# A two-layer hybrid trunk in fp32: five places where loads, transposes, decays, tokens and operand halves are reordered

## What is computed

```python
# layer 0
h = rmsnorm(x, even_norm_mix)
proj = h @ w_in                      # columns: bg, cg, hv, z, xbc, dt
y_a = bg * causal_dwconv(cg * hv, conv_w)
xbc = silu(causal_dwconv(xbc, ssd_conv_w) + ssd_conv_b)
dt = softplus(dt_raw + dt_bias); a = -exp(a_log)
y = ssd_scan(xs, dt, a, bm, cm) + d_skip * xs      # decays exp(cumsum(dt * a))
y_b = group_rmsnorm(y * silu(z)) * ssd_norm_g
x = x + concat(y_a, y_b) @ w_out
x = x + swiglu(rmsnorm(x, even_norm_ffn), w_gate, w_up, w_down)
# layer 1
x = x + diff_attention(rmsnorm(x, odd_norm_mix), ...)
h = rmsnorm(x, odd_norm_ffn)
logits = h @ w_router                # 8 experts, top 2 of them per token
x = x + sum over a token's two experts of gate * swiglu(h, w_e)
```

## Time and profile before

| | us |
|---|---|
| median of 3 runs | 2041.79 (2039.48 to 2042.93) |
| profiled execution, its own time | 2043.4 |
| its span, first to last instruction | 2041.6 |
| PE busy in it | 1971.8 (97%) |
| DVE, ACT, POOL busy | 749.8, 652.1, 490.9 |
| mean granted TensorE clock | 0.983 of full |

### The profile page before, as it was taken

How to read it: one execution, slowest core, us unless ns; L and a number is a source line. 1 busy time by engine, 2 the same in 40 slices (tenths; PEclk the granted TensorE clock), 3 DMA queues, 4 the chain that set the end, 5 groups by cost and what they waited for, 6 DMA issues and landing times.

```text
span 2041.6 us, 28889 instructions
## 1 busy us (share of the span) xinstructions
PE 1971.8 (97%) x11899; PEld 1731.5 (85%) x11899; DVE 749.8 (37%) x1138; ACT 652.1 (32%) x1061; POOL 490.9 (24%) x246
## 2 busy tenths in 40 slices
PE   7999999999999999998899999999999999999996
PEld 6787778888888888886688999999999999888885
DVE  4625564210010005948722000010010101989896
ACT  4333223232222224337630000000000011878784
POOL 3446664265445544540011000000000000000010
PEclk9999999999999999999898999999999999999998
DMA  7862222243233232330007977888888898999995
GB/s 241 298 197 74 63 73 93 73 124 93 92 95 103 88 105 75 101 104 1 22 1 268 322 241 260 300 299 302 276 305 288 284 312 278 377 372 374 361 396 212
DMA packets 295087, 405.38 MB, mean 199 GB/s; under 512 B 11264, under 2 KB 211018, under 8 KB 294954
## 3 DMA queue, kind: packets, MB, share of 16 engines
q1 hardware_dynamic: 292650, 395.11, 57.4%
q0 software_dynamic: 2304, 8.39, 1.1%
HBM read 372.67 MB, written 30.80 MB: 198 GB/s over the span
## 4 chain that ended last, share of the span: by engine, by line
PE 88%; DVE 3%; ACT 2%; DVEq 2%; POOL 2%; issue 1%; DMA 1%; SPq 0%; POOLq 0%; ACTq 0%
PE ps L1729 20%; PE ps L1736 10%; PE ps L375 5%; PE ps L376 5%; PE ps L377 5%; PE ps L393 5%; PE ps L394 5%; PE ps L395 5%; PE ps L1787 4%; PE ps L1789 4%; PE ps L1788 4%; PE ps L410 2%; PE ps L412 2%; PE ps L411 2%; DVEq L1186 1%
## 5 line engine op out<-in xcount | busy, mean ns | idle before, releaser
L1022 POOL TENSOR_TENSOR w_lo<-raw,w_hi 128x1024 fp32r<-128x1024 f32 (+1 forms) x159 | 390.3, 2463 | 462.7 <-ACT w_hi L758 462.7
L1563 DVE TENSOR_TENSOR s_lo<-s_raw,s_hi 128x1024 fp32r<-128x1024 f32 x198 | 236.9, 1222 | 28.1 <-ACT s_hi L1933 22.6
L2183 DVE TENSOR_TENSOR hid<-ps,silu_g 128x160 f32<-128x160 f32 x110 | 35.7, 324 | 550.1 <-ACT silu_g L1908 550.1
L1729 PE MATMUL ps<-xT,w_gate 128*128 128x132 f32 (+1 forms) x1760 | 226.6, 282 | 4.6 <-issue 4.0
L758 ACT ACTIVATE w_hi<-raw 128x1024 fp32r<-128x1024 f32 (+1 forms) x159 | 164.8, 1043 | 205.1 <-PE ps L395 136.4
L375 PE MATMUL ps<-act_a_hi,w_hi 128*128 128x512 f32 x568 | 226.3, 398 | 0.0
L1729 PE MATMUL ps<-xT,w_up 128*128 128x132 f32 (+1 forms) x1760 | 224.4, 281 | 0.0
L1908 ACT ACTIVATE silu_g<-ps 128x160 f32<-128x160 f32 x110 | 33.5, 304 | 593.3 <-PE ps L1729 593.3
L1933 ACT ACTIVATE s_hi<-s_raw 128x1024 fp32r<-128x1024 f32 x198 | 206.7, 1061 | 51.0 <-PE ps L1789 46.5
L377 PE MATMUL ps<-act_a_hi,w_lo 128*128 128x512 f32 x568 | 221.2, 389 | 0.0
L376 PE MATMUL ps<-act_a_lo,w_hi 128*128 128x512 f32 x568 | 221.1, 389 | 0.0
(11 more groups left out here) (355 smaller groups left out, 2949.1 us busy)
## 6 DMA issues: line engine op xcount, KB each, us to landing
w_gate<-in_moe_w_gate SPq DMA_DIRECT2D x55, 1024.0 KB, 5.6
w_up<-in_moe_w_up SPq DMA_DIRECT2D x55, 1024.0 KB, 8.5
w_down<-in_moe_w_down SPq DMA_DIRECT2D x55, 1024.0 KB, 11.0
s_raw<-in_moe_w_gate SPq DMA_DIRECT2D x33, 1024.0 KB, 7.6
s_raw<-in_moe_w_up SPq DMA_DIRECT2D x33, 1024.0 KB, 8.3
s_raw<-in_moe_w_down SPq DMA_DIRECT2D x33, 1024.0 KB, 7.7
raw<-in_even_w_in SPq DMA_DIRECT2D x43, 512.0 KB, 4.5
raw<-in_attn_w_qkv SPq DMA_DIRECT2D x24, 512.0 KB, 3.8
```

The lines of the kernel that those rows point to most:

```text
L1022: pool.tensor_tensor(w_lo[:, u % HL_SLOTS, 0:size(u)], raw[:, u % RAW_SLOTS, 0:size(u)], flat(w_hi[:, u % HL_SLOTS, 0:size(u)]), ALU.subtr ...
L1563: return eng.tensor_tensor(s_lo[u % S_HL][:], s_raw[u // 2 % S_RAW][:, u % 2, :], s_hi[u % S_HL][:].bitcast(F32), ALU.subtract)
L1729: mm = pe.matmul(ps[:, bank, i * CAP:i * CAP + width], w_slots[s][i][:, k, c:c + P], xT[:, k, 0:width], start=(k == 0), stop=(k == KD - 1))
```

## The change

**First loads.** Order now: tile 0 of x, gain, tile 1, units 0 and 1, the three `rows_sb` and three `small` loads, tile 2, unit 2, tile 3, unit 3. The transpose of `rows_sb` moves behind the two turns, ahead of unit 0's products, in another bank of PSUM (the accumulator memory); unit 3 waits until DVE has copied it. **Time steps.** The turn of `dt_rows` moves from ahead of the z units to between the first and the second. **Log decays.** `log_decays(c, 0)` and `(c, 1)` for c >= 1 move from the start of even a to the odd a before, ahead of `ssd_second`. **Home of the tokens.** `h_tok` moves to byte 81920 (that of `raw`), and other tiles are placed around it; DVE waits for all of `lo_done` before it writes there; SP's wait ahead of slot 3 goes, and a wait for the scatter comes one round later, ahead of the load of the next expert's rows; POOL's scatter waits for five hidden tiles and not three. **Last parts.** In the narrow passes the high and low parts of the last hidden chunk come right after its turn may be done, ahead of the parts of the weights that follow.

```diff
-    h_tok, _ = place("h_tok", [P, NT, D], F32, NT * D * 4)
+    h_tok, _ = place("h_tok", [P, NT, D], F32, 5 * NT * D * 4)
...
         load_x(0)
-        for src, r, n in rows:
-            sp.dma_start(rows_sb[r:r + n, :], src).then_inc(rows_in, 16)
         sp.dma_start(gain[:], gains[0][0].partition_broadcast(P)).then_inc(gain_in, 16)
         load_x(1)
-        for i, name in enumerate(("ssd_dt_bias", "ssd_a_log", "ssd_d")):
-            sp.dma_start(small[:, 16 * i:16 * i + 16], t[name][0].partition_broadcast(P)).then_inc(small_in, 16)
+
+        def load_rows_and_small():
...
         for u in range(N_UNITS):
             load(u)
-            if u < NT - 2:
-                load_x(2 + u)
+            if u == 1:
+                load_rows_and_small()
+            if 1 <= u < NT - 1:
+                load_x(1 + u)
...
         pe.wait_ge(masks_ready, 1)
-        pe.wait_ge(rows_in, 48)
-        pe.transpose(ps[:, 0, 0:N_ROWS], rows_sb[0:N_ROWS, :], ident[0:N_ROWS, 0:N_ROWS]).then_inc(rows_turned, 1)
-
-
         turn(0, 0, normed_tile(0))
         turn(0, 1, normed_tile(0))
-        first_features(0, U_XBC)
+
+        def turn_rows(i):
+            if i == 0:
+                pe.wait_ge(rows_in, 48)
+                pe.transpose(ps[:, 3, 0:N_ROWS], rows_sb[0:N_ROWS, :], ident[0:N_ROWS, 0:N_ROWS]).then_inc(rows_turned, 1)
+            if i == 3:
+                pe.wait_ge(rows_kept, 1)
+
+        first_features(0, U_XBC, turn_rows)
...
         feature_out(U_DT, 4, act_a_hi, act_a_lo)
-        pe.wait_ge(dt_evac, 1)
-        for tt in range(NT):
-            mm = pe.transpose(ps[:, 5, tt * P:(tt + 1) * P], dt_rows[:, tt * P:(tt + 1) * P], ident[:])
-        mm.then_inc(dt_turned, 1)
+
+        def turn_dt(i, tile):
+            if (i, tile) == (1, 0):
+                pe.wait_ge(dt_evac, 1)
+                for tt in range(NT):
+                    mm = pe.transpose(ps[:, 5, tt * P:(tt + 1) * P], dt_rows[:, tt * P:(tt + 1) * P], ident[:])
+                mm.then_inc(dt_turned, 1)
 
         pe.wait_ge(xbc_evac, XBC_TILES)
-        token_out(G_Z, U_Z, KD, of(act_a_hi, act_a_lo))
+        token_out(G_Z, U_Z, KD, of(act_a_hi, act_a_lo), turn_dt)
...
         for a in range(KD):
-            if a % 2 == 0:
-                log_decays(a // 2, 0)
-                log_decays(a // 2, 1)
+            if a == 0:
+                log_decays(0, 0)
+                log_decays(0, 1)
             low_parts(U_A + 3 * a + 2 + AHEAD)
             pool.wait_ge(ya_hi, a + 1)
             pool.tensor_tensor(act_b_lo[:, a, :], conv_acc, flat(act_b_hi[:, a, :]),
                                ALU.subtract).then_inc(ya_lo, 1)
+            if a % 2 and a < KD - 1:
+                log_decays(a // 2 + 1, 0)
+                log_decays(a // 2 + 1, 1)
             (ssd_second if a % 2 else ssd_first)(a // 2)
...
         dve.wait_ge(gain_in, 80)
+        dve.wait_ge(lo_done, N_UNITS)
         for tt in (0, 1):
             dve.wait_ge(tile_sum, 7 + tt)
...
                     sp.wait_ge(down_done, u - WSLOTS + 1)
-                if u == WSLOTS - 1:
-                    sp.wait_ge(scattered, 16 * 2 * NT)
-                    sp.wait_ge(picked, 3)
                 load_expert_round(sp, e, r, u % WSLOTS)
                 if r == WSLOTS:
+                    if w == 0:
+                        sp.wait_ge(scattered, 16 * 2 * NT)
                     sp.wait_ge(x_turned, w * 2 + 2)
...
                 if r == 2 and t + 1 < SMALL:
                     small_x_high(t + 1)
+                if r == S_CHUNKS - 1:
+                    high_parts(down_unit(t, r - 1) + S_AHEAD)
+                    hidden_high(r)
                 if r >= 1:
                     high_parts(down_unit(t, r - 1) + chunk_units(r - 1) - 1 + S_AHEAD)
-            hidden_high(S_CHUNKS - 1)
...
         pool.wait_ge(slots_made, 1)
-        pool.wait_ge(tile_done, 3)
+        pool.wait_ge(tile_done, 5)
```

More of the change, by code:

```diff
@@ L203, in build_trunk @@
     zero_ready, y_zeroed = sem("zero_ready"), sem("y_zeroed")
-    rows_turned = sem("rows_turned")
+    rows_turned, rows_kept = sem("rows_turned"), sem("rows_kept")
     rms_done, h_ready = sem("rms_done"), sem("h_ready")
@@ L314, in _ @@
         load_x(0)
-        for src, r, n in rows:
-            sp.dma_start(rows_sb[r:r + n, :], src).then_inc(rows_in, 16)
         sp.dma_start(gain[:], gains[0][0].partition_broadcast(P)).then_inc(gain_in, 16)
         load_x(1)
-        for i, name in enumerate(("ssd_dt_bias", "ssd_a_log", "ssd_d")):
-            sp.dma_start(small[:, 16 * i:16 * i + 16], t[name][0].partition_broadcast(P)).then_inc(small_in, 16)
+        def load_rows_and_small():
+            for src, r, n in rows:
+                sp.dma_start(rows_sb[r:r + n, :], src).then_inc(rows_in, 16)
+            for i, name in enumerate(("ssd_dt_bias", "ssd_a_log", "ssd_d")):
+                sp.dma_start(small[:, 16 * i:16 * i + 16], t[name][0].partition_broadcast(P)).then_inc(small_in, 16)
         def load(u):
@@ L1111, in norm @@
                                          ALU.mult).then_inc(h_ready, 1)
-                if n == 0 and tt == 1:
-                    dve.wait_ge(rows_turned, 1)
-                    dve.tensor_copy(cols[:, 0:N_ROWS], ps[:, 0, 0:N_ROWS])
                 if tt % 2:
@@ L1117, in norm @@
                     turned_low(n, tt, act_a_hi, act_a_lo)
+                if n == 0 and tt == 1:
+                    dve.wait_ge(rows_turned, 1)
+                    dve.tensor_copy(cols[:, 0:N_ROWS], ps[:, 3, 0:N_ROWS]).then_inc(rows_kept, 1)
         def turned_low(n, tt, hi, lo, scale=1.0):
@@ L1470, in build_experts @@
     xT_next, o = place("xT_next", [P, KD, CAP], F32, o)
+    yT, o = place("yT", [P, KD, CAP], F32, o)
+    assert o <= 5 * NT * D * 4
+    y_lower, o = place("y_lower", [P, NT, D], F32, 5 * NT * D * 4)
+    o_hid = o
     hid, o = place("hid", [P, FT, CAP], F32, o)
     silu_g, o = place("silu_g", [P, 2, CAP], F32, o)
-    place_no, o3 = place("place_no", [P, CAP], F32, scratch + 49152)
-    pick, _ = place("pick", [P, NT, CAP], F32, o3)
-    yT, o = place("yT", [P, KD, CAP], F32, o)
     x_rows, o = place("x_rows", [P, D], F32, o)
@@ L1480, in build_experts @@
     y_rows2, o = place("y_rows2_sb", [P, D], F32, o)
-    y_lower, o = place("y_lower", [P, NT, D], F32, o)
     assert o <= 8 * NT * D * 4
     y_higher, _ = place("y_higher", [P, NT, D], F32, NT * D * 4)
+    place_no, o3 = place("place_no", [P, CAP], F32, scratch + 49152)
+    pick, _ = place("pick", [P, NT, CAP], F32, o3)
     w_home = (scratch, scratch + 24576, NT * D * 4 + 24576, NT * D * 4)
@@ L1489, in build_experts @@
     s_lo = [place(f"s_lo{i}", [P, 1024], F32R, w_home[1 + i // 3] + 8192 * (i % 3) + 4096)[0] for i in range(S_HL)]
-    o_s = 4 * NT * D * 4
-    s_silu, o_s = place("s_silu", [P, 2, 512], F32, o_s)
+    s_silu, o_s = place("s_silu", [P, 2, 512], F32, 4 * NT * D * 4)
     s_hid, o_s = place("s_hid", [P, 2, 512], F32, o_s)
-    s_hid_hi, o_s = place("s_hid_hi", [P, 2, 512], F32R, o_s)
+    assert o_s <= 4 * NT * D * 4 + 2 * KD * CAP * 4
+    s_hid_hi, o_s = place("s_hid_hi", [P, 2, 512], F32R, o_hid)
     s_hid_lo, o_s = place("s_hid_lo", [P, 2, 512], F32R, o_s)
     s_x1_hi, o_s = place("s_x1_hi", [P, KD, P], F32R, o_s)
-    s_x1_lo, o_s = place("s_x1_lo", [P, KD, P], F32R, o_s)
-    assert o_s <= 4 * NT * D * 4 + (2 * KD + FT + 2) * CAP * 4
+    assert o_s <= o_hid + (FT + 2) * CAP * 4
+    s_x1_lo, _ = place("s_x1_lo", [P, KD, P], F32R, scratch + 65536 - D * 4)
     s_x0_hi, o_s = place("s_x0_hi", [P, KD, P], F32R, 8 * NT * D * 4)
@@ L2245, in small_pass @@
                     small_x_low(t + 1)
+                if r == S_CHUNKS - 1:
+                    low_parts(down_unit(t, r - 1) + S_AHEAD)
+                    hidden_low(r)
                 if r >= 1:
                     low_parts(down_unit(t, r - 1) + chunk_units(r - 1) - 1 + S_AHEAD)
-            hidden_low(S_CHUNKS - 1)
         def small_y_copy(t, h):
```

## The result

| | before | after |
|---|---|---|
| median of 4 runs each, us | 2041.72 (2039.48 to 2042.93) | 2022.97 (2022.49 to 2023.75) |
| profiled execution, its own time | 2043.4 | 2022.9 |
| its span | 2041.6 | 2021.0 |
| mean granted clock | 0.983 | 0.987 |

The ratio after to before is 0.9906, with a 95% interval of 0.9895 to 0.9918. Of before that is 19.2 us (16.7 to 21.4; the two medians themselves are 18.8 apart), and the kernel is faster by far more than the 4 us that a measurement can tell.

What follows compares the result with a forecast made beforehand. PE, busy 1971.8 of 2041.6 us, was taken as the bound, so only its waits and half clock could be won. Five terms summed to 19.1 us: 2024.3 from the profiled 2043.4, 2022.7 for the median, range 2018.0 to 2031.0.

Steps and rivals of the forecast that it cites:

- the head: Kernel start: reordered first loads let PE's first products start earlier; gain 1.6 us, bounds a 2.3 loss and 4.0.
- turn of dt: Time steps: 24 products of the first z unit cover PE's wait for `dt_rows`; 3.9 us plus 2.8 of clock, 6.7.
- first expert pass: Slot 3's load issued right behind slot 2's, so PE's stop goes; 3.99 us plus 2.4 of clock, 6.4.
- last hidden chunk: End of two narrow passes: PE's waits of 1.42 us go; gain 2.8 us, bounds 0 and 2.8.
- log decays: Chunks 2 and 3: without POOL's `dtri` pair, DVE's state update ends 0.8 us sooner each; gain 1.6 us.
- the clock term: 5.2 us lost at a granted clock of 0.50 behind the `dt_rows` and slot 3 stalls: 2.8 and 2.4.
- rival 5: PE's visible waits are not what limits; nothing but the expert stall is won: 2035.4 us; chance 0.04.
- Rival 4: Slower: SP's wait delays later loads if the scatter takes over 19.9 us, 39.0 to eat the gain; chance 0.03.
- The bound from below: In the head: SP held 3.91 us at the six small loads makes unit 2 later by 2.3 us, a loss.
- Rival 1: The clock gives less back at the two stalls, only the stalls go: 13.9 us won, 2027.9; chance 0.18.
- Rival 2: The expert stall only moves, as slot 3's or round 5's load is late: 6.4 us lost, 2029.1; chance 0.10.
- Rival 3: The head loses, SP held at an issue: 2.3 us lost and not 1.6 won, 2026.6; chance 0.05.

## Why the prediction was right, point by point

The forecast of 2022.7 was right by the measured 2022.97. Four of its five terms hold one by one; the head gave about half of its 1.6:

| term | forecast | alone, by the ratio | in the traces |
|---|---|---|---|
| turn of dt | 6.7 | 7.4 (4.5 to 10.0) | 6.8 |
| first expert pass | 6.4 | 6.5 (4.1 to 9.0) | 6.6 |
| last hidden chunk | 2.8 | 2.9 (1.0 to 4.7) | 2.8 |
| log decays | 1.6 | 2.5 (0.6 to 4.3) | 1.5 |
| head | 1.6 | 0.6 (-1.2 to 2.5) | 0.8 |
| sum | 19.1 | 19.9 | 18.5 |

(In the traces: before against after. The head is the shift of the dt unit's last product, 83.24 to 82.44; the turn of dt what passes from there to the first `dtri` wait, 77.5 and 70.8; the others as in the first section. With the 1.9 that no edit explains they make 20.4 of the span's 20.6.)

That the number came within 0.3 us is in part luck. The sum was taken off the profiled execution of before (2043.4), which gives 2024.3, and then 1.6 more went off because the median of before lies that much lower. But part of that distance is the clock term itself: a run of before with the shorter half clock behind its stalls (see below) has less to gain. After has no such stalls, and its median (2022.97) is no lower than its profiled execution (2022.87), so the 1.6 was not there to take. What made up for it are 1.9 us between attention and the experts that no edit gave. Two slips moved nothing: PE waits for |dt| three units behind its turn and not seven (DVE was done with it at 91.1, 13 us ahead), and rival 5's price was 6.4, under the "7 us or more" of all cases but the last.

**The turn of dt.** Right in both halves. The window of the earlier trace rows now reads:

```profile
86.50:93.20 6.70, 6.70 (x33) 5.55 (x32) 2.28 (x2) 2.17 (x3) 6.70 (x3) 1.00 0.76 253
```

The 24 products cover the copy with some to spare; twelve were 1.2 short, which puts the lateness at 3.8 to 3.9. The clock part was of the right kind but at its upper end. Between the stall's end and the next wait 73.3 us passed in before and 72.1 to 72.2 in the traces with the head alone, the decays alone and the last parts alone, where the half clock lasted 3.4 us and not 6.8. With the stall filled it was 70.6 (87.70 to 158.29), so the longer one cost 2.7 and the shorter about 1.5. The forecast took one execution, that of before, for all. This is what the Trainium skill, "TensorE: Matmul & The Clock Gate", section "What's actually happening", says of a start (the number of slow matmuls differs from run to run); here it is seen behind a stall, and the trace agrees. The expert stall does the same: 6.8 us in the traces of before, of the decays alone, of the last parts alone and of the wait put back, 3.4 in those of dt alone and of the head alone. It may account for a part of the spread of before (2038.8 to 2045.7 over all its runs), but that isn't shown: with both stalls filled eleven runs still spread from 2034.7 to 2038.7, and the half clock of attention and routing differs between executions too.

**The first expert pass.** Right in what goes. What moves in its place was right in direction and off in two sizes that cancel. SP's timeline in after:

```profile
1106.98 4.02 SPq L287 DMA_DIRECT2D w_down<-in_moe_w_down  x1
1129.28 0.35 SPq L1590 DMA_DIRECT2D x_rows<-h_slots  x1
...
1130.30 0.39 SPq L287 DMA_DIRECT2D w_gate<-in_moe_w_gate  x1
```

```profile
1110.15 1.16 POOL L2038 DMA_INDIRECT h_slots<-h_tok,idx  x1 [76.45 <-PE ps L1745]
```

From the scatter's start to SP's release it is 1129.28 - 1110.15 = 19.1 us, where the forecast took the 15.1 of before. The 15.1 is what it takes with SP held behind it (15.2 with the wait put back, 1097.31 to 1112.54); with round 4's loads issued ahead of it, it was 19.1 here and 18.9 with the home alone (1120.28 to 1139.15). But the `w_up` tile of round 5, issued at 1130.79, lands in 10.5 and not in 14.9, at 1141.3, and is wanted at 1143.99: 2.7 to spare, where 4.8 were forecast. (The 2.1 between them are mostly the next expert's rows and `w_gate`, 1.5 us of SP's queue ahead of `w_up`, which the forecast did not count.) Rival 4's first condition, a scatter of over 19.9 us, was thus missed by less than 1 us, its price by far.

**The last hidden chunk, the log decays.** Right, and the decays by what was named: DVE's state pair no longer runs beside POOL's pair, and is 0.75 us shorter.

**The head.** The weakest step, and the term that was mis-sized: 1.6 forecast, 0.8 between the two traces. Even that is within what executions differ by: the dt unit's last product came at 82.35 to 83.56 in the seven traces with the head of before and at 81.26 to 82.83 in the five with the head of after, 0.7 apart in the mean. The first product was to come near 15 us and came at 14.48; the turn of tile 2 near 21.8, and it came at 21.29, 2.1 earlier than before, but at half clock. The bound from below showed itself in part: SP was held for 3.64 us at the first of the small loads (1.18 at unit 1 before it). What failed is the hole: forecast 1 to 2 us and costed at nothing, it was 2.44 in after and 1.93 to 2.46 in the three kernels made from after that keep its head, and the clock fell to 0.50 behind all four. Window of after:

```profile
20.80:24.10 3.30, 2.81 (x13) 2.82 (x14) 2.66 (x5) 1.50 (x4) 0.00 (x0) 0.50 1.14 355
```

13 instructions there, where the window behind it, 0.1 us longer, has 31 at full clock; the eight transposes of the turn took 1.97 us, and 1.03 in the run with the square first. And the forecast put the hole down to the landing of unit 2, without asking why ACT takes the square of tile 2 behind the rounding of it. That order, not the load, was the limit, as the run with the square first shows.

**The rivals.** Rival 1 fell by the filled stalls; it was right only in that the loss is smaller in some runs. Rival 2 did not come, though it was close with the scatter left where it was. Rival 3: by the ratio of the head alone a small loss is not excluded, by the traces it is a small gain. Rivals 4 and 5 did not come.

## What to carry to other kernels

A stall of TensorE of about 4 us cost its width here and 0.4 to 0.7 of it more in half clock behind it (1.5 to 2.7 us for 3.9), a wait of 1.2 little more than its width; so the long ones are worth removing first, and where one can't be removed, products that nobody uses got the second part back (5.5 us for the two stalls). When a wait is dropped because its buffer moved, look at what then runs beside the load that it used to hold: here the scatter ate all 9.3 us of the cover where it was left in its place. And before a hole is put down to a load, look at what the engine that makes the operand did while it was idle.

## What was not expected of the hardware

- One and the same stall has 6.8 us at half clock behind it in one execution and 3.4 in another, with nothing else changed ahead of it.
- A load of 1 MB took 23.1 us to land with the eight indirect transfers of the scatter beside it, and 13.8 without, although the DMA engines moved more with it than without. Windows of the kernel with the earlier scatter, and of after:

```profile
1105.00:1110.00 5.00, 5.00 (x39) 5.00 (x38) 0.00 (x0) 0.00 (x0) 2.61 (x3) 1.00 1.03 408
```

```profile
1105.00:1110.00 5.00, 5.00 (x39) 5.00 (x38) 0.33 (x1) 0.30 (x1) 0.00 (x0) 1.00 1.06 378
```

- In the head of after the DMA engines were nearly idle while the loads of 64 bytes for every partition (`small`) were on their way, with 4 KB loads queued behind them:

```profile
11.00:13.00 2.00, 1.88 (x8) 1.48 (x8) 1.29 (x2) 2.00 (x5) 2.00 (x1) 1.00 0.27 39
```

- Between 925 and 1093 us, in attention and routing, after gained 1.9 us on before: half clock from 1063 to 1083 in before and from 1055 to 1069 in after. No edit gave it. From attention's first long wait to the first product of the experts it is 169.0 us in before and 167.1 in after, and in the six kernels whose program is that of before in this stretch it lies anywhere from 166.7 (both kernels with filled stalls) to 169.0 (the decays alone); with the new home alone it is 169.0. What decides it in an execution stays open.
